# One low-part subtraction moved by a step, and the first odd gather moved behind a block's end, in a mixture-of-experts decoder layer

## The reference

```python
    scores = jax.nn.sigmoid(hf.astype(f32) @ w_router.astype(f32))
    ...
    wts = wts / wts.sum(-1, keepdims=True) * ROUTED_SCALE
    ...
    def body(acc, blk):
        toks, bw, e = blk
        xb = hp[toks]
        yb = (jax.nn.silu(xb @ w_gate[e]) * (xb @ w_up[e])) @ w_down[e]
        return acc.at[toks].add(yb.astype(f32) * bw[:, None]), None
```

## Time and profile before

| what | value |
|---|---|
| time, median of 3 runs (lowest to highest) | 2500.54 us (2498.16 to 2504.78) |
| time of the profiled execution | 2502.44 us |
| its span in the profile | 2500.6 us |
| mean granted TensorE clock | 0.976 of full |
| busy: PE, DVE, ACT, POOL | 94%, 66%, 51%, 39% of the span |

### The profile page before, as it was taken

One profiled execution on the slowest core, in us unless ns is written; L12 is line 12 of the kernel. 1 busy time (PEld: TensorE's weight loads), 2 busy tenths in 40 slices (PEclk: granted clock), 3 DMA queues, 4 the chain that ended last, 5 costly groups with the idle time before them and its releaser, 6 DMA issues. The chain is left out here.

```text
span 2500.6 us, 49354 instructions
## 1 busy us (share of the span) xinstructions
PE 2345.8 (94%) x11266; PEld 1900.4 (76%) x11268; DVE 1659.6 (66%) x2220; ACT 1263.4 (51%) x2025; POOL 980.9 (39%) x772
## 2 busy tenths in 40 slices
PE   8899999989998799999999999999999999999966
PEld 6576777668886677888778887787878888887844
DVE  6685867758877766666666666656666657656337
ACT  4525253532325655555555555555655556655334
POOL 0010101011110155555555555555645556655437
PEclk9999999989998899999999999999999999999989
DMA  7243434465656479888897878888888789987796
GB/s 253 76 168 122 136 118 144 135 223 187 226 204 210 157 240 279 242 231 255 273 269 230 262 222 259 263 266 262 268 254 236 222 252 290 272 271 213 177 248 202
DMA packets 165327, 551.13 MB, mean 220 GB/s; under 512 B 31344, under 2 KB 56080, under 8 KB 144784
## 3 DMA queue, kind: packets, MB, share of 16 engines
q1 hardware_dynamic: 109696, 355.03, 39.9%
q0 software_dynamic: 54960, 195.27, 32.6%
q10 hardware_dynamic: 608, 0.02, 0.0%
HBM read 394.99 MB, written 155.25 MB: 220 GB/s over the span
## 5 line engine op out<-in xcount | busy, mean ns | idle before, releaser
L2645 PE MATMUL psG<-gu_split,xT_hi 128*128 x2624 | 626.2, 391 | 3.4 <-ACT xT_hi L2421 1.9
L2645 PEld LDWEIGHTS psG<-gu_split,xT_hi 128*128 128x128 f32 x2624 | 495.0, 189 | 107.6 <-issue 4.1
L1669 POOL DMA_INDIRECT xg<-hcut,gi x332 | 418.4, 1260 | 201.5 <-ACT gi L2432 113.9
L2659 PE MATMUL psG<-gu_split,xT_lo 128*128 x1304 | 342.3, 404 | 0.9 <-issue 0.9
L2590 DVE TENSOR_TENSOR HT_lo<-psH,HT_hi 128x256 fp32r<-128x256 f32 x162 | 68.7, 424 | 379.6 <-ACT HT_hi L2489 371.3
L2528 DVE TENSOR_TENSOR gu_split<-raw_gu,gu_split (+1 forms) x127 | 284.3, 2281 | 44.7 <-issue 27.0
L2659 PEld LDWEIGHTS psG<-gu_split,xT_lo 128*128 128x128 f32 x1304 | 232.9, 188 | 44.6 <-issue 2.5
L2406 POOL DMA_INDIRECT acc<-y,si x81 | 184.4, 2277 | 160.2 <-ACT y L2498 146.3
L2444 ACT ACTIVATE gu_split<-raw_gu x126 | 234.5, 1909 | 25.0 <-issue 18.3
L2697 PE MATMUL psY<-d_hi,HT_lo 128*128 x648 | 202.9, 394 | 31.7 <-DVE HT_lo L2590 31.5
L2489 ACT ACTIVATE HT_hi<-psH 128x256 fp32r<-128x256 f32 x162 | 62.2, 384 | 286.6 <-PE psH L2666 261.4
(11 more groups left out here) (404 smaller groups left out, 4102.5 us busy)
## 6 DMA issues: line engine op xcount, KB each, us to landing
raw_gu<-in_w_gate_dram SPq DMA_DIRECT2D x64, 1024.0 KB
raw_gu<-in_w_up_dram SPq DMA_DIRECT2D x64, 1024.0 KB
raw_d<-in_w_down_dram SPq DMA_DIRECT2D x64, 1024.0 KB
wring<-split_d SPq DMA_DIRECT2D x24, 1024.0 KB, 5.7
second<-blank SPq DMA_DIRECT2D x17, 512.0 KB, 6.7
split_d<-wring POOLq DMA_DIRECT2D x8, 1024.0 KB, 4.2
raw_d<-mixed SPq DMA_DIRECT2D x16, 512.0 KB, 5.6
xt<-in_x_dram SPq DMA_DIRECT2D x16, 512.0 KB, 5.7
```

Of the source, the lines that this page charges most:

```text
L1669: nc.gpsimd.indirect_dma_start(out=to[:, g, 0:PIECE], out_offset=None, in_=hcut.rearrange("r a w -> (r a) w"), in_offset=bass.IndirectOffs ...
L2645: nc.tensor.matmul(psG[slot][:], xT_hi[slot][:, c, :], right[:, bass.ds(w, 1), c, :].rearrange("p a n -> p (a n)"), start=(n == 0 and c == ...
L2659: m = nc.tensor.matmul(psG[slot][:], xT_lo[slot][:, c, :], gu_hi[:, bass.ds(w, 1), c, :].rearrange("p a n -> p (a n)"), start=False, stop= ...
```

## The change

Four things, all in the order of instructions. `split(words[n + 2], 1)` at the end of VectorE's step becomes `split(words[n + 1], 1)` behind `HT_lo` of the following step. The 16 operations for `pidx` leave VectorE; ScalarE makes them at the end of the placing block, with a per-partition bias tile `piece` that VectorE fills by four memsets early in that block. POOL waits for them at the placing block's end and issues the first odd gather as the first thing of the expert block. The order of everything else on an engine stays.

```diff
--- before.py
+++ after.py
@@ -1767,6 +1767,9 @@
         hot_s = sem("hot_s")
         disp_s = sem("disp_s")
         idx_s = sem("idx_s")
+        pidx_s = sem("pidx_s")
+        piece_s = sem("piece_s")
+        piece = sb("piece", [P, 1])
 
         d_pieces = [(raw_d[:, 1, c, :], s_d[:, 0, c, :], s_d[:, 1, c, :]) for c in range(FE // P)]
         PIECES = len(d_pieces)
@@ -1844,10 +1847,7 @@
             nc.gpsimd.tensor_copy(gi[0][:], idx[:, 0:1]).then_inc(gi_s, 1)
             pool.wait_ge(gi_s, 1)
             gather_rows(nc, htab, xg[0], gi[0], x_in[0])
-            pool.wait_ge(idx_s, 3)
-            nc.gpsimd.tensor_copy(gi[1][:], pidx[:, 0, :]).then_inc(gi_s, 1)
-            pool.wait_ge(gi_s, 2)
-            gather_pieces(nc, hcut, xg[1], gi[1], x_in[1])
+            pool.wait_ge(pidx_s, 1)
 
         @block.scalar
         def _(act):
@@ -1917,6 +1917,15 @@
                 if n == EARLY - 3:
                     for t in dispatched(n + 1):
                         places(t)
+            act.wait_ge(idx_s, 2)
+            act.wait_ge(piece_s, QUADS)
+            odd = idx[:].rearrange("p (b k) -> p b k", k=2)[:, :, 1]
+            for a in range(QUADS):
+                at = slice(a * QP, (a + 1) * QP)
+                for g in range(QUADS):
+                    last = nc.scalar.activation(pidx[at, :, g], odd[g * QP:(g + 1) * QP], ACT.Identity, scale=float(QUADS),
+                                                bias=piece[at, :])
+            last.then_inc(pidx_s, 1)
 
         @block.vector
         def _(dve):
@@ -1997,13 +2006,6 @@
                 nc.vector.tensor_tensor(idx[:, 0:BLOCKS], none[:], some[:], ALU.add).then_inc(idx_s, 1)
                 nc.vector.tensor_scalar(idx[:, BLOCKS:WORDS], zr[:, 0:AHEAD], blockno[:, 0:1], float(SEQ), ALU.add,
                                         ALU.add).then_inc(idx_s, 1)
-                dve.wait_ge(idx_s, 2)
-                odd = idx[:].rearrange("p (b k) -> p b k", k=2)[:, :, 1]
-                for a in range(QUADS):
-                    for g in range(QUADS):
-                        last = nc.vector.tensor_scalar(pidx[a * QP:(a + 1) * QP, :, g], odd[g * QP:(g + 1) * QP], float(QUADS), float(a),
-                                                       ALU.mult, ALU.add)
-                last.then_inc(idx_s, 1)
 
             def ranks_of_used():
                 link(nc.vector.tensor_scalar(used[:], nb[:], 0.0, None, ALU.is_gt))
@@ -2071,6 +2073,8 @@
             low(3)
             dve.wait_ge(zeroed, 1)
             nc.vector.tensor_copy(zr[:], zeros[:, 0:BLOCKS]).then_inc(zr_s, 1)
+            for a in range(QUADS):
+                nc.vector.memset(piece[a * QP:(a + 1) * QP, :], float(a)).then_inc(piece_s, 1)
             positions()
             for n in range(EARLY):
                 if n:
@@ -2369,6 +2373,9 @@
 
         @block.gpsimd
         def _(pool):
+            nc.gpsimd.tensor_copy(gi[1][:], pidx[:, 0, :]).then_inc(gi_s, 1)
+            pool.wait_ge(gi_s, 2)
+            gather_pieces(nc, hcut, xg[1], gi[1], x_in[1])
             for k in range(2):
                 if k == 0:
                     pool.wait_ge(turned[1], 1)
@@ -2580,7 +2587,6 @@
             low_x(1, 1)
             when_first(dve, block0, lambda: split(block0, 1))
             when_first(dve, block1, lambda: split(block1, 0))
-            when_first(dve, block1, lambda: split(block1, 1))
 
             def body(i):
                 words = entries(dve, i * TURN, TURN + 2)
@@ -2589,6 +2595,7 @@
                     s.wait(dve, HThi_s)
                     nc.vector.tensor_tensor(HT_lo[:], psH[:, 0:FE].rearrange("p (a b) -> p a b", a=2), HT_hi[:],
                                             ALU.subtract).then_inc(HTlo_s, 1)
+                    when_first(dve, words[n + 1], lambda: split(words[n + 1], 1))
                     when_first(dve, words[n], lambda: split(words[n], 2))
                     low_x(s.turn + 2, k)
                     s.wait(dve, H_s)
@@ -2599,7 +2606,6 @@
                     if k == 0:
                         turn_x(s.turn + 2)
                     when_first(dve, words[n + 2], lambda: split(words[n + 2], 0))
-                    when_first(dve, words[n + 2], lambda: split(words[n + 2], 1))
 
             turns(dve, body)
 
```

## The result

| | before | with the change |
|---|---|---|
| median | 2500.1 us (4 runs, 2498.2 to 2504.8) | **2457.5** us (4 runs, 2453.8 to 2461.4) |
| ratio | | 0.9827 [0.9805, 0.9849] |
| profiled execution; its span | 2502.4, 2500.6 | 2459.5, 2457.6 |
| first to last `psH` of the expert loop | 1491.6 | 1453.6 |
| TensorE waits for `HT_lo` | 31.5, 21 times | 1.6, 4 times |

The account below looks back on a forecast made before the run. TensorE, busy for 94% of the span, was taken as the bound, so only its idle time could be won. Terms -30.0 and +0.6 gave -29.4: profiled execution 2473.0 us, median 2471, range 2461 to 2484.

Parts of the forecast that it names:

- part 1: Expert loop: moving the up half's subtraction behind `HT_lo` removes TensorE's stall; net -30.0 us, bounds -36.3 and -18.4.
- the ceiling of 36.3: Expert loop: the most to be won, 31.5 us of `HT_lo` waits plus 0.23 refill in each of 21 turns.
- the 6.3 that were to return: Formerly stalled turns: gathers landing later than wanted give back 0.3 us per turn, 6.3 in all, bounds 0 to 17.9.
- The threshold of 2.75: Expert loop: TensorE could go on without waiting if `HT_lo` ended 2.75 us after `psH`.
- its 0.85: Formerly stalled turns: the most that returns per turn if the gather sets when the transposes start, 0.85 us.
- rival (b): Expert loop: nothing returns, gathers land in time everywhere; -36.3 and nothing from the other parts, 2464 us; chance 0.2.
- parts 2 and 3: Placing block's end and first odd gather: 2.6 us won and lost again, net +0.6, bounds -2.6 and +3.
- the 6.1 that I called the most: Placing block's end: ScalarE's 16 small activations take 6.1 us at most, at 0.384 each, and end in time.
- the 4 that I took: Expert block's start: the first odd gather's rows land 4 us after the last issue, between 0 and 5.2.
- who pays: The loop's other turns: later H, with 1.8 us free in an odd step, and later weight loads cost 0.
- rival (d): Expert loop: VectorE is held up just as long, the stall moves to `turn_H`'s wait for H; about 2486 us; chance 0.08.
- Rival (c): Turns splitting in their odd step: later pair weights delay the even gather, TensorE's row transposes wait; about 2508 us; chance 0.03.

Follow-up runs that it names:

- split_only: The kernel before with only the loop's move of the up half's subtraction behind `HT_lo`, without the handover part: 2458.3 us, ratio 0.984.
- both_halves: The change with both halves of the gate and up subtractions behind `HT_lo`: 2512.3 us, ratio 1.0043.
- split_wait: split_only with SyncE's weight loads of the expert block held until the first odd gather has landed: 2457.5 us, ratio 0.9923.
- behind_rows5: The change with the moved subtraction behind the low part of the rows instead of ahead of it, repeated with more timed runs: 2459.1 us.
- both_turn4: both_halves with the loops written out for four steps per turn instead of two: 2502.7 us in one run, with two empty steps.

## Why the prediction was right and wrong

**Right: what bounds the kernel and what frees it.** The wait for `HT_lo` fell from 31.5 to 1.6, and `split_only` alone has the whole gain. Of the 36 turns that start behind an even split most take 17.84 to 17.89 and not 19.32; six take 18.2 to 18.9.

**Wrong in size: part 1, -30.0, of which the loop gave -38.0.** This is the step that failed, and both of its terms were off: the ceiling of 36.3 was too low, and the 6.3 that were to return were too much. The ceiling was 31.5 of recorded waits and 0.23 for each of 21. By the lengths of the odd steps there were 40.7 us to win. Six more steps, with an `HT_lo` that ended 3.0 after `psH` and no wait in the list, were 0.3 longer each. In one stalled step, at 2275.74, the granted clock fell to 0.5 for 3.4 us behind the wait (0.57 on average from 2281 to 2285), which cost 1.6. The rest is a refill of 0.27 and not 0.23. The threshold of 2.75 for `HT_lo` itself holds: in the change the late ones, 2.97 to 3.52 after `psH`, cost 0.23 to 0.80, what they lie beyond it.

The return was 3.4 and not 6.3 (bounds 0 to 17.9; by the prediction's own terms its 0.85 is 16.46 + 2.30 + 2.25 + 0.42 - 17.87 - 2.75 = 0.81). The step took the 16.46 us from `psH` to the transposes in the earlier trace rows for the time that a gather needs. There it was the time of a gather held up: POOL's four issues ended 11.27 after `psH`, stretched under VectorE's two adjacent subtractions. Ten of the 26 turns that split in their odd step waited so before, up to 3.8. In the change none does; a turn like the earlier trace rows, whose odd `psH` is at 2057.35:

```profile
2066.72 0.95 POOL L1669 DMA_INDIRECT xg<-hcut,gi  x1 [0.30 <-issue]
```
```profile
2071.98 2.15 DVE L2519 STREAM_TRANSPOSE xF<-xg 128x1024 f32<-128x1024 f32 x1
```

The issues end 10.32 after `psH`, and the transposes start at 14.63, unhindered. But the gather is the limit in some of the turns that the forecast was about, those with an even split. There the last issue ends 8.7 to 9.8 and the transposes start 14.9 to 16.8 after `psH`. VectorE's waits for the odd rows, 17.9 us in 20 places with a longest of 1.7 (34.6, 11 and 3.8 before), now lie in turns without a split in their odd step. In six turns the next `HT_lo` was late by it, as in the rows of 1248.11 above: 3.3 us. So what I described does happen, but in six places and not in 21, and with half of the sum; rival (b), by which nothing returns, is nearer in its total than in its mechanism.

**Wrong in size: parts 2 and 3, +0.6.** They came to -0.5 (34.8 to 34.3), by errors that nearly cancelled. ScalarE's sixteen activations take 7.59 and not the 6.1 that I called the most; an upper bound from a wider tile was none: the 98 int32 columns of this form take 0.46 us, the 256 columns of `HT_hi` 0.384. They end at 858.65, 3.6 us after the start of VectorE's last `finish`, so the barrier opens later than that work would allow. VectorE's own part came 4.65 earlier and not 2.6, and the index copy took 0.18 and not 2.3: it got in 0.95 before the subtraction (859.26 and 860.21). The Trainium skill ("SBUF — State Buffer", section "Who interferes with whom") says that whoever is issued first has the port, and the trace agrees, with 0.18; the gather behind it paid in its place, 2.09. The rows came 6.0 after the last issue (865.84 to 871.85, with the gather's last signal at 871.72), beyond the 4 that I took. Before the change, without the weight loads beside it, that signal came 1.9 after the last issue (863.57 to 865.51).

**Right by luck: "who pays", cost 0.** The 1.8 us that H was to have free are counted against `psH`, and TensorE's sequencer needs H about 2 us before the even `psH`. The change leaves it 1.95 at the least; `both_halves` shows what lies beyond, in rival (d)'s place: 45.0 us.

**Rival (c) exists, in small.** Six even steps of the change have their low pass 0.3 to 0.6 late and are 3.2 us longer in all, with H in time. In the worst but one of them, POOL and TensorE:

```profile
1138.26 0.99 POOL L1662 DMA_INDIRECT xg<-htab,gi  x1 [0.55 <-issue]
```
```profile
1149.69 0.38 PE L2672 MATMUL psH<-ident,H 128*128 128x128 f32 x2
...
1151.44 0.96 PE L2665 MATMUL psG<-gu_split,xT_lo 128*128 x3 [0.38 <-issue]
```

H ended at 1147.26. Behind its wait for H the sequencer waits for the even gather, issued at 1138.26 in a turn with an odd split, and the last signal of that gather is recorded at 1148.44, 10.2 later and 1.25 before `psH`. That alone is not enough: in six more turns the signal comes 1.30 to 1.57 before `psH` and the low pass is on time. What parts them is the load of the table behind this wait, 1.0 us in all six late turns (1.25 to 1.54) and 0.33 to 0.34 in the six that are on time. In the kernel before no such signal comes later than 2.77 before `psH`. So the moved half delays pair weights and gather, as the rival said, and again the edge lies a good microsecond ahead of the use that I measured to.

**The sum.** Forecast 2471 and measured 2457.5, 13.5 apart in the profiles as in the medians: 4.4 by the ceiling, 2.9 that did not return, 0.6 in the even steps, 1.1 at the handover, and 4.5 ahead of `idx`, which is spread. The repeat at 2464.1 shows what that spread is worth. My range of 2461 to 2484 ended at rival (b)'s total and had no room for a low ceiling or for the spread.

**Of the gain.** Of the 43 us, some 24 hang on the session: where the kernel before takes 2477, `split_wait` and `behind_rows5`, which both move the half and were timed over several runs, win 17.6 to 19. The change itself was not timed there. What its order removes even there is the stall, 19.1 us.

## What to carry to other kernels

When a late engine is relieved, ask of each bound that you read beside it whether the same lateness made it, and in which kind of turn you read it. Take what can be won from the lengths of the steps and not from the list of waits, which leaves out the steps that are late by less than it shows. Count the margin of a value not to the instruction that reads it but to the moment at which the reader's sequencer has to run ahead again, above all where a loop's end follows. And before a small stall is called a property of the kernel, profile the unchanged kernel a second time.

## What the hardware showed that was not expected

**A longer loop body can cost far more than it saves.** `turn4` (the change, four steps per turn) lost some 285 us beside the time of its two empty steps: 221 in the loop, 57 between the loop and the last block, the rest ahead of `idx`. VectorE's waits, and the row of the instruction queue (packets, MB, share):

```profile
DVE HT_lo L2596 <- issue: 376.1, 40, 11.2
```
```profile
q14 instruction: 264, 2.16, 0.3%
```

against this row of `both_turn4`, whose loop has the same operations in another order, with one conditional subtraction fewer ahead of the loop:

```profile
q14 instruction: 28, 0.23, 0.0%
```

At each of 40 turns VectorE stood 9.4 us on average with nothing to wait for (TensorE's step there grew by 5.7), and the packets rose by 236, six per turn: the body is fetched anew in every turn, as it seems. What decides it, where the body lies or the order within it, was not tried by itself, nor how long a body may be. The Trainium skill ("Runtime: NRT & Kernel Launch", section "Instruction fetch mechanics") says that a taken branch to a target outside the instructions held must fetch first; the trace is in line with that, with 9.4 us and six packets a turn; it doesn't show the fetch as such.

**Subtractions hold up GpSimd's gathers.** In the change an issue of `xg` from `hcut` takes 0.94 to 0.96 alone and up to 3.06 where a subtraction of a weight's low part (two inputs in SBUF) runs beside it, the scatter 1.6 alone and up to 3.7. Of the 122 issues with a subtraction beside them 27 still took under 1.05, and 25 of these had started 0.25 to 0.5 ahead of it. Three of the four of one turn:

```profile
1198.13 1.06 POOL L1669 DMA_INDIRECT xg<-hcut,gi  x1 [0.55 <-issue]
1199.50 2.18 POOL L1669 DMA_INDIRECT xg<-hcut,gi  x1 [0.30 <-issue]
1201.99 0.95 POOL L1669 DMA_INDIRECT xg<-hcut,gi  x1 [0.31 <-issue]
```

**A transfer share of 0.98 costs TensorE little.** Through 63.5 us at 297 GB/s (above) it lost 0.17 us, and from 1195.5 to 1268.2, at a share of 0.98 and 299 GB/s, 0.66 of 72.7, behind two waits of VectorE for its rows of 1.1 and 1.4. The earlier trace rows had let me take 0.96 for the edge.

**Signals can be late.** TensorE's signal to ScalarE came 0.5 to 2.5 us late in 37 turns of one session and in no turn of another, the program being the same. It is shown by the semaphore's record and by when `HT_hi` starts; its cause is open.
